# A hybrid decoder trunk in fp32 on one core: the first weight sum of each down projection made by two adding DMA transfers instead of GpSimd

## The reference

```
h = rms_norm(x, g[4])
f = jnp.square(jax.nn.relu(h @ w_up[l])) @ w_down[l]
x = x + rms_norm(f, g[5])
```

## Time and profile before

| | before |
|---|---|
| median of 3 runs | 1481.64 us (1481.55 to 1481.72) |
| the profiled execution's own time | 1484.23 us |
| its span in the trace | 1482.1 us |
| granted PE clock, mean | 0.998 |
| busy: PE, DVE, ACT, POOL | 1463.4, 896.6, 633.6, 381.8 us |
| HBM read, written | 160.87 MB, 6.29 MB |

### The profile page before, as it was taken

The page is one execution under the profiler, slowest core; times in us unless marked ns, Lnnn a source line. Parts: engine busy times, 40 slices in busy tenths (PEclk is TensorE's granted clock), DMA queues, the critical chain, the costliest instruction groups (busy, mean ns, idle before and its releaser), DMA issues.

```text
span 1482.1 us, 19058 instructions
## 1 busy us (share of the span) xinstructions
PE 1463.4 (99%) x7810; PEld 1258.9 (85%) x7810; DVE 896.6 (60%) x1045; ACT 633.6 (43%) x877; POOL 381.8 (26%) x272
## 2 busy tenths in 40 slices
PE   9999999999999999999999999999999999999997
PEld 7978998889888888888898889988898988888886
DVE  6345554846467566575982464747466584757659
ACT  6335433634444343343562454325444342534344
POOL 2001820300171513315030028102002805151422
PEclk9999999999999999999999999999999999999999
DMA  8532132421324325152353233134203352423402
GB/s 285 179 94 94 58 128 85 160 96 57 114 86 142 114 94 162 57 170 100 114 192 121 65 97 124 58 113 170 86 29 114 115 169 86 141 87 119 137 29 100
DMA packets 83959, 168.40 MB, mean 114 GB/s; under 512 B 3744, under 2 KB 19872, under 8 KB 82848
## 3 DMA queue, kind: packets, MB, share of 16 engines
q1 hardware_dynamic: 82432, 164.90, 33.2%
q10 hardware_dynamic: 1440, 2.27, 0.4%
HBM read 160.87 MB, written 6.29 MB: 113 GB/s over the span
## 4 chain that ended last, share of the span: by engine, by line
PE 91%; DVE 4%; ACT 2%; issue 1%; DMA 1%; POOL 1%; POOLq 0%; SPq 0%; DVEq 0%; ACTq 0%
PE proj L748 25%; PE proj L750 25%; PE proj L749 25%; PE work L748 3%; PE work L750 3%; PE work L749 3%; PE work L777 2%; DVE w_lo L1492 1%; PE work L813 1%; PE work L823 1%; PE work L803 1%; ACT w_hi L1169 1%; PE work L905 1%; DMA w_raw<-in_w_up_dram 1%; PE work L884 0%
## 5 line engine op out<-in xcount | busy, mean ns | idle before, releaser
L1492 DVE TENSOR_TENSOR w_lo<-w_raw,w_hi 128x2048 fp32r<-128x2048 f32 (+1 forms) x103 | 235.6, 2287 | 253.4 <-ACT w_hi L1169 253.3
L748 PE MATMUL proj<-hT_hi,w_hi 128*128 128x512 f32 (+1 forms) x800 | 298.8, 374 | 2.1 <-DVE u L1528 2.1
L750 PE MATMUL proj<-hT_hi,w_lo 128*128 128x512 f32 (+1 forms) x800 | 297.7, 372 | 0.0
L749 PE MATMUL proj<-hT_lo,w_hi 128*128 128x512 f32 (+1 forms) x800 | 297.7, 372 | 0.0
L1169 ACT ACTIVATE w_hi<-w_raw 128x2048 fp32r<-128x2048 f32 (+1 forms) x103 | 185.2, 1798 | 235.1 <-PE proj L750 221.7
L748 PE MATMUL proj<-w_hi,hT_hi 128*128 128x512 f32 (+1 forms) x640 | 237.9, 372 | 1.1 <-DVE hT_lo L1684 1.1
L750 PE MATMUL proj<-w_hi,hT_lo 128*128 128x512 f32 (+1 forms) x640 | 232.2, 363 | 0.0
L749 PE MATMUL proj<-w_lo,hT_hi 128*128 128x512 f32 (+1 forms) x640 | 231.9, 362 | 0.0
L748 PEld LDWEIGHTS proj<-hT_hi,w_hi 128*128 128x128 f32 x800 | 150.7, 188 | 28.5 <-DVE w_lo L1492 2.7
L750 PEld LDWEIGHTS proj<-hT_hi,w_lo 128*128 128x128 f32 x800 | 150.7, 188 | 26.3
L749 PEld LDWEIGHTS proj<-hT_lo,w_hi 128*128 128x128 f32 x800 | 150.7, 188 | 25.9
(11 more groups left out here) (213 smaller groups left out, 2521.9 us busy)
## 6 DMA issues: line engine op xcount, KB each, us to landing
w_raw<-in_w_up_dram SPq DMA_DIRECT2D x32, 1024.0 KB, 5.6
w_more<-in_w_down_dram SPq DMA_DIRECT2D x24, 1024.0 KB, 5.1
w_raw<-in_w_in_dram SPq DMA_DIRECT2D x28, 768.0 KB, 4.4
w_raw<-in_x_wkv_dram SPq DMA_DIRECT2D x15, 1024.0 KB, 5.1
w_raw<-in_w_out_dram SPq DMA_DIRECT2D x8, 1024.0 KB, 5.2
w_raw<-in_x_wq_dram SPq DMA_DIRECT2D x8, 1024.0 KB, 5.0
w_raw<-in_x_wo_dram SPq DMA_DIRECT2D x8, 1024.0 KB, 5.0
w_hs<-in_w_down_dram SPq DMA_DIRECT2D x8, 1024.0 KB, 5.0
```

What stands on the lines that cost most here:

```text
L748: nc.tensor.matmul(dst, l_hi, r_hi, start=first, stop=False, skip_group_check=more)
L749: nc.tensor.matmul(dst, l_hi, r_lo, start=False, stop=False, skip_group_check=more)
L750: return nc.tensor.matmul(dst, l_lo, r_hi, start=False, stop=last, skip_group_check=more)
L1492: nc.vector.tensor_tensor(w_lo[:, slot, :, 0:cols], w_raw[:, raw, :, 0:cols], w_hi[:, slot, :, 0:cols].bitcast(F32), ALU.subtract).then_in ...
```

## The change

In each of the eight groups, POOL no longer adds b12 to b22 with two instructions. It issues two transfers from `w_down` in device memory, of half a block (512 KiB) each, that read b12's numbers a second time and add them to b22 in SBUF. They count on a new semaphore, `b_added`, 16 for each transfer. POOL then waits for both before s2, and ACT waits for `b_added` before it splits s1 for m5. The counts of `t_made` fall from 8 to 6 for each group.

```diff
-        t_made = counted("t_made", 8 * GROUPS)
+        t_made = counted("t_made", 6 * GROUPS)
+        b_added = counted("b_added", 32 * GROUPS)
...
+                elif name == "m5":
+                    act.wait_ge(b_added, nth(b_added, l, 32 * (g + 1)))
                 else:
-                    act.wait_ge(t_made, nth(t_made, l, 8 * g + {"m5": 2, "m6": 4, "m7": 6, "m3": 8}[name]))
+                    act.wait_ge(t_made, nth(t_made, l, 6 * g + {"m6": 2, "m7": 4, "m3": 6}[name]))
...
+                first = g * (FF // GROUPS)
+                for h, k in enumerate(halves):
+                    half = first + h * BK // 2 * P
+                    nc.gpsimd.dma_start(b22[:, k], w_down[l, half:half + BK // 2 * P, 512:D].rearrange("(k p) c -> p k c", p=P),
+                                        accum_op=ALU.add).then_inc(b_added, 16)
+
+                loaded(3)
+                pool.wait_ge(b_added, nth(b_added, l, 32 * (g + 1)))
                 for k in halves:
-                    nc.gpsimd.tensor_tensor(b22[:, k], b12[:, k], b22[:, k], ALU.add).then_inc(t_made, 1)
-
-                loaded(3)
-                for h, k in enumerate(halves):
-                    made(h + 1)
                     nc.gpsimd.tensor_tensor(s2[:, k], b22[:, k], b11[:, k], ALU.subtract).then_inc(t_made, 1)
```

More of the change, by code:

```diff
@@ L614, in b21_free @@
                 split_of(l, g, "m2")
-                sp.wait_ge(t_made, nth(t_made, l, 8 * g + 8))
+                sp.wait_ge(t_made, nth(t_made, l, 6 * g + 6))
             def load_group(l, g):
@@ L634, in load_group @@
                     split_of(l, g, "m1")
-                    sp.wait_ge(t_made, nth(t_made, l, 8 * g + 6))
+                    sp.wait_ge(t_made, nth(t_made, l, 6 * g + 4))
                     load_down(l, g + 1, w_hs[:], 0, 0, q_loaded[3])
@@ L2093, in made @@
                 def made(n):
-                    pool.wait_ge(t_made, nth(t_made, l, 8 * g + n))
+                    pool.wait_ge(t_made, nth(t_made, l, 6 * g + n))
                 def rows_read(g, name):
@@ L2109, in mlp_group @@
                     pool.wait_ge(w_lo_done, nth(w_lo_done, l, group_block(g, 0) + 1))
+                first = g * (FF // GROUPS)
[5 more added lines that the diff above has]
+                pool.wait_ge(b_added, nth(b_added, l, 32 * (g + 1)))
                 for k in halves:
-                    nc.gpsimd.tensor_tensor(b22[:, k], b12[:, k], b22[:, k], ALU.add).then_inc(t_made, 1)
-                loaded(3)
-                for h, k in enumerate(halves):
-                    made(h + 1)
                     nc.gpsimd.tensor_tensor(s2[:, k], b22[:, k], b11[:, k], ALU.subtract).then_inc(t_made, 1)
-                made(4)
+                made(2)
                 for k in halves:
```

## The result

The changed kernel takes **1492.86 us** (median of 4 runs, 1492.08 to 1493.94) against 1481.60 us: a ratio of 1.0076, with a 95% interval of 1.0059 to 1.0094. That is 11.3 us slower. The forecast was 1491.0 us, between 1482.5 and 1499. The size came out, but by another road than the prediction took.

What follows compares the result with a forecast made beforehand. PE was taken as the bound, busy 1463.4 of 1482.1 us. Up block 2's lateness cost 3.9 us in layer 0 and 3.5 in layer 1, plus 2.0 for the clock: 9.4, so 1491 us, range 1482.5 to 1499.

Steps and rivals of the forecast that it cites:

- the late up block 2: First group of each layer: adding transfers share the full DMA engines, block lands 3.9 us late, PE loses 3.9 and 3.5.
- the free wait for `b_added`: POOL's queue: `b_added` after 13 us in first groups, 8 to 9 in others, about 20 allowed before cost; priced at nothing.
- What goes: Two POOL additions per group, 4.75 us a pair, 38.0 us over eight, off PE's path; at most 1.6 us gained, layer 0.
- The price of a transfer: DMA engine time of each group's 1.05 MB of adding transfers: 3.9 us, between 2.6 and 5.2.
- my upper end: DMA engines, each group: an adding transfer also reads its destination, handling up to twice the bytes, 5.2 us.
- my first rival: Hidden anyway: up block 2 not late, `b_added` within 20 us, time within 0.2%, 1479 to 1484.6 us; chance 0.20.
- my third rival: Adding at a quarter rate or less: ACT late for ReLUs everywhere, up block 2 late; 1502 us up; 0.10 with long clock fall.
- my signs of being wrong: Profile after: up block 2 landing as before, ACT waiting for a5 or s1, or PE waiting somewhere no step names.
- The clock: PE's idle time in both layers' first groups may halve its clock: 2 us together, from nothing to some 3 us each.
- The other groups at nothing: Six later groups: up block 2 has 6.2 us of slack at ACT, covering 3.9 and 5.2, so no price.

Runs made afterwards that it cites:

- e4: Changed kernel with adding transfers only in groups 2 to 4 of each layer, POOL's additions kept in the first: 1482.00 us, ratio 1.0003.
- e5: Changed kernel with POOL's two transfers plain, overwriting b22 instead of adding, same size, queue and order: 1483.53 us, ratio 1.0013.
- e8: Changed kernel with descriptor room 1280, a5 ahead of the `b_added` wait, and first-group transfers issued without waiting for `hT_lo`: 1491.75 us, ratio 1.0070.
- e1: Changed kernel with 1280 bytes of descriptor room a partition in place of 1024: 1488.90 us, ratio 1.0048.
- e3: Changed kernel with POOL making a5 ahead of its wait for `b_added` in each layer's first group: 1483.40 us, ratio 1.0010.
- e6: Changed kernel with first-group transfers issued earlier, without the wait for `hT_lo`: 1484.00 us, ratio 1.0025.

## Why the prediction came out as it did

Two steps failed, the late up block 2 and the free wait for `b_added`; I take the terms in the order of the prediction.

**What goes: right.** Removing POOL's additions gained nothing that can be measured (e4, in six groups). In the change POOL was idle beside `w_lo` of up block 2 in layer 0, and `w_lo` took 2.29 us in place of 4.21, but PE had no wait left there to gain from.

**The price of a transfer: too low.** I took 3.9 us of the engines for a group, between 2.6 and 5.2; the profile gives 6.3. The factor of two for the second read, my upper end, was right (2.0, and e5 shows it by taking the adding away). The base was off: I took the rate of full windows, and the packets' own time is 3.1 us for 1.05 MB. The Trainium skill ("Collectives: The Full Stack", on why ReduceScatter is half of AllGather) has the second source read halve the rate. The traces agree with it: the same bytes took 3.4% adding and 1.6% plain.

**Up block 2 late by 3.9 us, PE by 3.9 and 3.5: failed in the change.** It landed 7.9 and 8.2 us after its issue (9.2 and 7.3 before) and PE didn't wait for it. I had the adding data start 2 us after POOL does and share evenly. The windows after say otherwise, to set beside the earlier trace rows. Below them are the queues' packets, MB and share, from 424 to 429 us (first line) and from 429 to 430:

```profile
428.00:429.00 1.00, 1.00 (x11) 1.00 (x10) 0.00 (x0) 0.00 (x0) 0.00 (x0) 1.00 1.05 379
429.00:430.00 1.00, 1.00 (x10) 1.00 (x10) 0.00 (x0) 0.00 (x0) 0.00 (x0) 1.00 1.18 311
430.00:431.00 1.00, 1.00 (x11) 1.00 (x10) 0.00 (x0) 0.00 (x0) 0.00 (x0) 1.00 0.94 209
...
q1 hardware_dynamic: 922, 1.86, 99.8%
...
q1 hardware_dynamic: 140, 0.26, 79.4%
q0 software_dynamic: 26, 0.05, 38.3%
```

Until 429 the engines move SP's data alone, at 379 to 412 GB/s from 425 on; the first packets of POOL's queue come only then, some 4.5 us after the start of POOL's issue. By then up block 2 was nearly in: it landed at 430.6. The same delay holds for plain transfers (e5, 4 us) and in layer 1 (4.5 us). Where nothing of SP's was under way it was 2 us, as I had taken it: for the second transfer of this group and for the first of e8. So the late start goes with SP's loads ahead of it, not with the adding. That is half of my first rival, up block 2 not late. Up block 3 took the delay (12.0 us to land, 10.5 before), and it had slack. The mechanism is real: e8 moves the issue 5 us up and up block 2 is late by 3.9 and 4.5 us. In the change it didn't act.

**The wait for `b_added`, "I cost this wait at nothing": the step that failed.** Both of its numbers were off. I expected 13 us and it was 18.2, since the second issue waited until the first transfer had landed. Nothing in the trace of before could show that; I had not asked what room the descriptors have, though the number 1024 stands in the kernel.

And I allowed 20 us. From POOL's start at 424.5 ACT's wish at 449.6 is 25.1 us off, not 28: I had taken it from a run with 2.3 us of wait ahead of it. I added 3.9 us for a delay that didn't come, and 6 for gaps between the ReLUs, where the trace gives 7.2 - 3.7 = 3.5 (the burst of ReLUs and squares takes time itself). POOL's three sums took 14.1 us, 2 less than I took. So 25.1 - 14.1 + 3.5 = 14.5 us were free, and 18.2 - 14.5 = 3.7 us is PE's wait. That sum closes by itself, since the 3.5 us are read from the same wait; what tests them is that ACT's wait less PE's is 3.5 us again in layer 1 (7.0 - 3.5), in e1 (6.0 - 2.5) and in layer 1 of e5 (4.4 - 0.9).

What came about is the end of my third rival, "the chain behind `b_added`", without its condition: adding ran at half the plain rate, not at a quarter, and up block 2 was not late. It began to cost at 14.5 us, where I had set the point at 20, and only in the two first groups. ACT waiting for a5 and up block 2 landing as before were both among my signs of being wrong, and both showed.

**The clock: right in kind.** I took 2 us for both layers; the profiled run has some 3 us, all in layer 1. Of the timed runs of the change two have a mean clock of 0.996 and two of 0.994, and those are the slower ones (1493.3 and 1493.9 against 1492.1 and 1492.4).

**The other groups at nothing: right**, by e4.

So 3.9 + 3.5 + 2.0 = 9.4 us was forecast at up block 2, and 3.7 + 3.5 + 3 = 10 us was paid at m1. That the two sums are close is luck; without the trace and e3 the total would have looked like a proof of the wrong step.

What stays open: how the room is used up. A room of 1280 held two adding transfers in every group, one of 1024 in none, but two plain ones in five groups of eight and up to three adding quarters. Why POOL's data starts later when SP's loads are under way: whether it is served behind them or its issue takes longer, no run separates. And what e6's three slow runs waited for.

## What to carry to other kernels

Replacing an engine's instruction by a transfer also replaces its place in that engine's order: what costs is all that stands behind the new wait, so price the last thing in that queue that somebody waits for (here a5), and move it ahead of the wait if it doesn't depend on it. Take slack from a run at the median time, and count only the part of a gap that the burst after it leaves. A total that agrees doesn't show where the time went; look for the predicted wait at its own place.

## What the runs showed of the hardware that I had not expected

- An adding transfer from device memory into SBUF took twice the engine time and nearly twice the packets of a plain one of the same bytes: 3.4% and 4352 against 1.6% and 2304.
- With 1024 as the room for descriptors, POOL stood 7 to 9 us before it issued a second adding transfer of 512 KiB, in every group, until the first had landed; with 1280 it followed at once.
- Data of a POOL transfer began some 4 to 4.5 us after the start of its issue beside SP's loads, adding or plain, and 2 us after it with SP's queue empty (435.06 to 437 in the change, 419.5 to 421.5 in e8).
- PE idle for 3.5 us was followed by 6.8 us at a granted clock of 0.50 in layer 1, and 3.7 us idle by none in layer 0 of the same run. In e8, 2.8 us idle were followed by 3.4 us at 0.50.
- POOL's pair of subtractions (128x1024 each) took 4.75 us alone and 6.80 beside a DVE subtraction, and that one (128x2048) 2.29 us alone and up to 4.50 beside POOL's.
